# Removing the two zero columns between and behind the token streams: 384 columns instead of 386, and outer convolution taps per stream

## What is computed

```python
def depthwise_conv(x, w, b):                    # x (batch, tokens, channels), zero padding at both ends
    k = w.shape[0]
    left = (k - 1) // 2
    y = lax.conv_general_dilated(x, w[:, None, :], window_strides=(1,),
                                 padding=[(left, k - 1 - left)], feature_group_count=x.shape[-1], ...)
    return y + b

def conv_ffn(h, w_in, dw, dw_b, w_out):         # all four layers, 3 taps, 1024 -> 2 x 2816 -> 1024
    u = depthwise_conv(h @ w_in, dw, dw_b)
    return (jax.nn.silu(u[..., :FFN_DIM]) * u[..., FFN_DIM:]) @ w_out

def ssd_mixer(h, ...):                          # layer 1, 3 taps
    proj = h @ w_in
    xbc = jax.nn.silu(depthwise_conv(proj[..., SSD_D_INNER:SSD_D_INNER + SSD_CONV_DIM], conv_w, conv_b))
    ...
```

## Time and profile before

| | |
|---|---|
| median of 3 runs | 1994.08 us (1992.12 to 1994.34) |
| the profiled execution, its own time | 1993.56 us |
| its span in the trace | 1991.8 us |
| PE busy | 1925.1 us, 97% of the span |
| DVE, ACT, POOL busy | 58%, 47%, 35% |
| mean granted TensorE clock | 0.988 |

### The profile page before, as it was taken

How to read it: one execution, slowest core, us unless ns; L and a number is a source line. 1 busy time by engine, 2 the same in 40 slices (tenths; PEclk the granted TensorE clock), 3 DMA queues, 4 the chain that set the end, 5 groups by cost and what they waited for, 6 DMA issues and landing times.

```text
span 1991.8 us, 30109 instructions
## 1 busy us (share of the span) xinstructions
PE 1925.1 (97%) x11802; PEld 1712.5 (86%) x11802; DVE 1153.4 (58%) x1803; ACT 926.5 (47%) x1575; POOL 697.6 (35%) x507
## 2 busy tenths in 40 slices
PE   5899999999998989999999999999999999999998
PEld 4789998799996767999987967899987977899986
DVE  3657751666626675777714953777723564777722
ACT  3534442544547645544425335544424454544422
POOL 0233334333335553323343741333243521323342
PEclk8999999999999999999999998999999999999999
DMA  9774356543240137634375664634364613443342
GB/s 395 315 271 137 127 183 231 179 119 125 92 135 28 49 138 297 211 119 125 101 259 180 206 184 190 235 125 128 117 219 165 230 39 117 138 123 122 127 127 74
DMA packets 80139, 322.74 MB, mean 162 GB/s; under 512 B 8976, under 2 KB 17664, under 8 KB 66688
## 3 DMA queue, kind: packets, MB, share of 16 engines
q1 hardware_dynamic: 78496, 318.93, 46.7%
q10 hardware_dynamic: 1504, 1.91, 0.3%
HBM read 315.70 MB, written 5.10 MB: 161 GB/s over the span
## 4 chain that ended last, share of the span: by engine, by line
PE 89%; DMA 3%; DVE 3%; issue 2%; ACT 2%; POOL 1%; SPq 0%; DVEq 0%; POOLq 0%; ACTq 0%
PE pair L1968 18%; PE pair L1970 18%; PE pair L1969 18%; PE pair L2001 8%; PE pair L2002 8%; PE pair L2003 8%; DMA mod_base<-in_w_mod 2%; PE pair L2122 2%; PE pair L1935 2%; PE pair L2216 1%; DMA mod_more<-in_w_mod 1%; PE pair L2127 1%; PE pair L1957 1%; PE pair L2136 1%; PE pair L2376 1%
## 5 line engine op out<-in xcount | busy, mean ns | idle before, releaser
L813 POOL TENSOR_TENSOR w_lo<-raw,w_hi 128x512 fp32r<-128x512 f32 (+1 forms) x375 | 588.8, 1572 | 1074.0 <-ACT w_hi L947 1073.9
L1968 PE MATMUL pair<-h_hi,w_hi 128*128 128x386 f32 (+1 forms) x2008 | 688.5, 343 | 3.8 <-DVE h_lo L1467 3.8
L1970 PE MATMUL pair<-h_hi,w_lo 128*128 128x386 f32 (+1 forms) x2008 | 682.9, 340 | 0.0
L1969 PE MATMUL pair<-h_lo,w_hi 128*128 128x386 f32 (+1 forms) x2008 | 682.2, 340 | 0.0
L1361 DVE TENSOR_TENSOR w_lo<-raw,w_hi 128x512 fp32r<-128x512 f32 x339 | 404.3, 1195 | 326.6 <-ACT w_hi L947 326.3
L947 ACT ACTIVATE w_hi<-raw 128x1024 fp32r<-128x1024 f32 x375 | 392.2, 1050 | 281.4 <-PE pair L2003 224.5
L1968 PEld LDWEIGHTS pair<-h_hi,w_hi 128*128 128x128 f32 (+1 forms) x2008 | 380.5, 189 | 12.3 <-issue 11.3
L1969 PEld LDWEIGHTS pair<-h_lo,w_hi 128*128 128x128 f32 (+1 forms) x2008 | 381.0, 190 | 0.5
L1970 PEld LDWEIGHTS pair<-h_hi,w_lo 128*128 128x128 f32 (+1 forms) x2008 | 380.2, 189 | 0.3
L1526 DVE SCALAR_TENSOR_TENSOR acc<-pair,taps,acc 128x385 f32<-128x385 f32 x176 | 108.9, 619 | 202.2 <-ACT acc L1061 202.2
L1061 ACT ACTIVATE acc<-pair,taps 128x386 f32<-128x386 f32 x176 | 117.1, 665 | 217.8 <-PE pair L1970 217.8
(11 more groups left out here) (308 smaller groups left out, 2083.0 us busy)
## 6 DMA issues: line engine op xcount, KB each, us to landing
raw<-in_ffn_in SPq DMA_DIRECT2D x176, 512.0 KB, 3.5
raw<-in_ffn_out SPq DMA_DIRECT2D x88, 512.0 KB, 3.6
mod_raw<-in_w_mod SPq DMA_DIRECT2D x36, 1024.0 KB, 7.1
mod_base<-in_w_mod SPq DMA_DIRECT2D x31, 1024.0 KB, 7.2
mod_more<-in_w_mod SPq DMA_DIRECT2D x18, 1024.0 KB, 21.7
raw<-in_ssd_conv SPq DMA_DIRECT2D x32, 512.0 KB, 3.5
raw<-in_ssd_z SPq DMA_DIRECT2D x16, 512.0 KB, 3.5
raw<-in_ssd_out SPq DMA_DIRECT2D x16, 512.0 KB, 3.5
```

The source lines that it names most:

```text
L813: pool.tensor_tensor(w_lo[:, m % SLOTS, 0:w], raw[:, m % SLOTS, 0:w], w_hi[:, m % SLOTS, 0:w].bitcast(F32), ALU.subtract).then_inc(w_low_p ...
L1968: ten.matmul(to, wh, h_hi[:, k, cols], start=k == 0, stop=False, skip_group_check=True)
L1969: ten.matmul(to, wh, h_lo[:, k, cols], start=False, stop=False, skip_group_check=True)
L1970: ins = ten.matmul(to, wl, h_hi[:, k, cols], start=False, stop=k == KD - 1, skip_group_check=True)
```

## The change

The two zero columns go: `LAT0` is `CTX`, `COLS` is 384, `AT` is 0, 128, 256. Every row of activations, every stream of `tile` and every instruction over a whole row is 384 columns wide; a row of four-byte values is 1536 bytes long, where it was 1544. With no zero between the streams, each outer tap is written for each stream by itself: two instructions over 127 and 255 columns in place of one over 385. The pooling matrices lose the column for the gap, and the four small writes of zeros at the start go.

```diff
-LAT0 = CTX + 1
-COLS = CTX + 1 + LAT + 1
+LAT0 = CTX
+COLS = CTX + LAT
...
             act.wait_ge(cond_loaded, 16)
-            act.wait_ge(vec_init, 2)
+            act.wait_ge(vec_init, 1)
...
                     vec.wait_ge(acc_ready, c + 1)
-                    vec.scalar_tensor_tensor(out=acc[:, j % 4, 1:COLS], in0=b[:, 0:COLS - 1], scalar=taps[:, l, j, 0:1],
-                                             in1=acc[:, j % 4, 1:COLS], op0=ALU.mult, op1=ALU.add).then_inc(tap_first, 1)
+                    for c0, w, _ in STREAMS:
+                        ins = vec.scalar_tensor_tensor(out=acc[:, j % 4, c0 + 1:c0 + w], in0=b[:, c0:c0 + w - 1],
+                                                       scalar=taps[:, l, j, 0:1], in1=acc[:, j % 4, c0 + 1:c0 + w], op0=ALU.mult,
+                                                       op1=ALU.add)
+                    ins.then_inc(tap_first, 1)
...
                     vec.wait_ge(tap_first, c + 1)
-                    vec.scalar_tensor_tensor(out=acc[:, j % 4, 0:COLS - 1], in0=b[:, 1:COLS], scalar=taps[:, l, j, 2:3],
-                                             in1=acc[:, j % 4, 0:COLS - 1], op0=ALU.mult, op1=ALU.add).then_inc(conv_done, 1)
+                    for c0, w, _ in STREAMS:
+                        ins = vec.scalar_tensor_tensor(out=acc[:, j % 4, c0:c0 + w - 1], in0=b[:, c0 + 1:c0 + w],
+                                                       scalar=taps[:, l, j, 2:3], in1=acc[:, j % 4, c0:c0 + w - 1], op0=ALU.mult,
+                                                       op1=ALU.add)
+                    ins.then_inc(conv_done, 1)
...
             vec.memset(cond32[:, :, :], 0.0).then_inc(vec_init, 1)
-            vec.memset(h_hi[:, :, CTX:LAT0].bitcast(F32), 0.0)
-            vec.memset(h_hi[:, :, COLS - 1:COLS].bitcast(F32), 0.0)
-            vec.memset(h_lo[:, :, CTX:LAT0].bitcast(F32), 0.0)
-            vec.memset(h_lo[:, :, COLS - 1:COLS].bitcast(F32), 0.0).then_inc(vec_init, 1)
```

More of the change, by code:

```diff
@@ L1555, in ssd_conv @@
                     vec.wait_ge(acc_ready, c + 1)
-                    vec.scalar_tensor_tensor(out=xbc[:, j, 1:COLS], in0=b[:, 0:COLS - 1], scalar=ssd_taps[:, j, 0:1],
-                                             in1=xbc[:, j, 1:COLS], op0=ALU.mult, op1=ALU.add).then_inc(tap_first, 1)
-                    vec.wait_ge(tap_first, c + 1)
-                    vec.scalar_tensor_tensor(out=xbc[:, j, 0:COLS - 1], in0=b[:, 1:COLS], scalar=ssd_taps[:, j, 2:3],
-                                             in1=xbc[:, j, 0:COLS - 1], op0=ALU.mult, op1=ALU.add).then_inc(conv_done, 1)
+                    for c0, w, _ in STREAMS:
+                        ins = vec.scalar_tensor_tensor(out=xbc[:, j, c0 + 1:c0 + w], in0=b[:, c0:c0 + w - 1],
+                                                       scalar=ssd_taps[:, j, 0:1], in1=xbc[:, j, c0 + 1:c0 + w], op0=ALU.mult,
+                                                       op1=ALU.add)
+                    ins.then_inc(tap_first, 1)
+                    vec.wait_ge(tap_first, c + 1)
+                    for c0, w, _ in STREAMS:
+                        ins = vec.scalar_tensor_tensor(out=xbc[:, j, c0:c0 + w - 1], in0=b[:, c0 + 1:c0 + w],
+                                                       scalar=ssd_taps[:, j, 2:3], in1=xbc[:, j, c0:c0 + w - 1], op0=ALU.mult,
+                                                       op1=ALU.add)
+                    ins.then_inc(conv_done, 1)
                     low_to(s.n0 + j + 5)
@@ L1781, in normed @@
                                                        scalar=attn_tab[:, g:g + 1],
-                                                       in1=bank(6 + i % 2)[:, col - (col > 0):col - (col > 0) + w],
+                                                       in1=bank(6 + i % 2)[:, col:col + w],
                                                        op0=ALU.mult, op1=ALU.mult)
@@ L2511, in pool_matrices @@
         for n in (CTX, LAT):
-            f = np.zeros((n, n + 1), np.float32)
+            f = np.zeros((n, n), np.float32)
             for t in range(n):
```

## The result

The changed kernel takes 1959.32 us (median of 4 runs, 1959.02 to 1961.35), the kernel before beside it 1994.21 us (1992.12 to 1994.51). The ratio is 0.9827, with a 95% interval of 0.9815 to 0.9839: 34.9 us faster. The forecast was 11.3 us, and its range ended at 1979.0. The direction was right, the size a third of what came.

The account below looks back on a forecast made before the run. PE was taken to bound the kernel, more than half through products of `tile`. Narrower products give 11.3 us, split taps on DVE 0, so 1994.08 becomes 1982.8 us; range 1979 to 1993.

Parts of the forecast that it names:

- PE bounds the kernel: Whole kernel: PE busy 97% of the span; 6024 tile products at 177.2 ns from start to start make 54%.
- The stationary pieces of `out_part` start elsewhere in a row: Products of `out_part`: their stationary operands begin at other places, count and width unchanged, claimed worth 0.
- The width term: Products of `tile`: streaming 384 columns instead of 386 saves 1.88 ns each, over 6024 products 11.3 us.
- the step would then be 175.35: Products of `tile`: start-to-start time at 384 columns, claimed to fall from 177.23 to 175.35 ns.
- The line through 256 and 512 columns: PE products: price of 0.4465 ns a column from two full widths; 386 columns measured 1.0 ns above it.
- Pieces of 16 bytes: Streams of `tile`: 386 columns cost as if fetched four columns at a time, the last fetch half empty.
- DVE hidden: Outer taps on DVE: splitting adds 0.12 to 0.20 us a tap, 50 to 83 us, none of it lengthening the kernel.
- The idle time of 1.22 us: DVE's wait before every second tile, claimed to fall from 1.22 to about 0.65 us and not to nothing.
- the margin forecast as 0.19 us or more: End of `ffn_in`: time left between the last tile's second tap and PE needing that bank, from 0.59 us before.
- the case of DVE as the bound: Rival: a tap split costing over 0.28 us makes DVE and ACT slower than PE; 2024 us, chance 0.06.
- only the slope: Rival: in `tile` the 1.0 ns excess stays, two columns save 5.3 us, giving 1988.8 us; chance 0.27.
- the step stays: Rival: 24 loads and their place beside the streams set a tile's pace; 1994 us within a few, chance 0.15.

## Why the prediction was wrong, point by point

**PE bounds the kernel, and the step from start to start is its price**: right. Both terms of the gain, and the loss of nearly every experiment, come out of steps times counts.

**"The stationary pieces of `out_part` start elsewhere in a row, with nothing in their count or width changed: 0"**: wrong, and the larger of the misses, 12.4 us. The count of a kind of product and its width were taken for all that its price can hang on. The earlier trace rows had shown a step of the same width that was 1.1 ns shorter, and I used that only as doubt about the tile; after the change the same half-wide tile takes 173.1 ns, and the difference is 0.2. The run with rows of `g` 385 columns apart shows that the row length alone makes 226.8 or 232.8 ns.

**The width term, 1.88 ns, 11.3 us**: the size came out, 1.95 ns with rows and places of before and 2.2 on average with all alike, but that was in good part luck. It was worked out as the distance to a line that was no floor (next point), from a cost paid in every product; with all alike 386 columns cost 0.1 ns in one tile and 4.3 in the next.

**That the step would then be 175.35**: wrong by 2.0 ns, 12 us. The line through 256 and 512 columns was taken as the floor, but both of its points had been measured in the kernel before, where operands did not lie alike. After the change the 512-wide step is 226.8 and the settled 256-wide one 120.0 (118.2 before), and (226.8 - 120.0) / 256 = 0.417 ns is the cycle of a 2.4 GHz clock. On that line 384 columns are 173.4, what was measured. The 0.4465 ns a column of the prediction held 5.7 ns of misplacement at its upper end, and its lower end was 1.8 ns too fast. I did note that rows of 1544 bytes begin at odd places, but as another name for the same 1.0 ns above the line, not as a cost of its own.

**Pieces of 16 bytes**: not what the place is about. The Trainium skill (SBUF — State Buffer, Specifications (TRN2)) has lines of 16 bytes; rows of 388 columns keep to them in every place and still take 174.7 ns where 173.4 was to be had. For the width, the alternating tiles of 386 columns speak against a half-empty last piece; 384, 256 and 512 are multiples of many things, and 386 is the only other width that ran, so what makes a width good stays open.

**DVE hidden**: right. The timeline of DVE over two tiles of the first `ffn_in`, which answers to the earlier trace rows:

```profile
261.76 0.74 DVE L1527 SCALAR_TENSOR_TENSOR acc<-pair,taps,acc 128x127 f32<-128x127 f32 x2 [1.15 <-ACT acc L1061]
262.41 0.55 DVE L1533 TENSOR_TENSOR g<-gate,g 128x384 fp32r<-128x384 f32 x1
262.88 0.74 DVE L1537 SCALAR_TENSOR_TENSOR acc<-pair,taps,acc 128x127 f32<-128x127 f32 x2
263.53 1.14 DVE L1361 TENSOR_TENSOR w_lo<-raw,w_hi 128x512 fp32r<-128x512 f32 x1
265.62 0.74 DVE L1527 SCALAR_TENSOR_TENSOR acc<-pair,taps,acc 128x127 f32<-128x127 f32 x2 [0.96 <-ACT acc L1061]
```

A split tap takes 0.65 us to the next start, as the pooling pair had said (0.66). The idle time of 1.22 us went to 0.96, not to 0.65: four taps take some 0.48 us and the faster PE 0.19, but `w_lo` gives 0.40 back. It takes 1.40 us in the odd tile of a pair, where it took 1.64, and 1.14 in the even one, where it took 1.30. Over the run `w_lo` on DVE fell from 403.8 to 362.3 us, which is why DVE's busy time rose by 9.7 us and not by the 50 to 83 of the prediction; without it the rise is 51. In the run with unsplit taps it is 404.9 us again, so the gain comes with the split; how was not shown. At the end of `ffn_in` the margin forecast as 0.19 us or more is there, PE first and then DVE:

```profile
273.04 0.39 PE L2009 MATMUL pair<-w_hi,g 128*128 128x512 f32 x1
...
275.80 0.39 PE L2009 MATMUL pair<-w_hi,g 128*128 128x512 f32 x1
```

```profile
274.72 0.74 DVE L1537 SCALAR_TENSOR_TENSOR acc<-pair,taps,acc 128x127 f32<-128x127 f32 x2
```

The last tap ends at 275.46, and c = 0 begins at 275.80, 2.76 us after the first product of `ffn_out` (forecast 2.78). The taps of both streams in one instruction gave the same time, so the case of DVE as the bound is out.

**The rivals and the range**: "only the slope" and "the step stays" both fell, on the other side. What was missing is a rival below the forecast. I had the mechanism in hand: the rival of the unchanged step speaks of 24 loads "and their place beside the streams" and says that such an effect "can go either way". But I gave the side of a larger gain 2 in 100 and priced the effect for tiles alone. The same 1.1 ns of the earlier trace rows over all 8184 products would have put 9 us below the forecast into the range, and the true time still more than 14 us outside it.

## What to carry to other kernels

When a change alters the length of a row or of a buffer, it moves every operand behind it; list where the operands of the costliest products begin, relative to each other modulo 256 bytes, before and after, and count a few ns for each product either way. Where single steps of a product stream scattered in a fixed pattern (177.2, 176.0, 175.6 ns), an even pace of 173.4 was to be had, and a line drawn through scattered steps was no floor; an even pace need not be the floor either (120.0 and 113.3 ns for 256 columns). Rows whose length is a multiple of 256 bytes, with all operand buffers at one offset, were as good as any arrangement tried here for products of 384 and 512 columns and for the whole kernel, and a pad of 64 bytes is a cheap way to find out. Read single steps too and not their mean alone: a mean of 175.6 was 173.5 and 177.6 by turns.

## What the runs showed of the hardware that I had not expected

- Two unused pads of 64 bytes between operand buffers cost 15.6 us of 1959 (0.8%); moving only the weights by 128 bytes cost 28.1 us (1.4%); moving everything by 64 cost nothing.
- With all operands alike, a product took its columns at 2.4 GHz plus 13.3 to 13.4 ns, at 256, 384 and 512 columns; with the weights 192 bytes ahead, one of 256 took 6.7 ns more than its columns. The Trainium skill (TensorE: Matmul & The Clock Gate, Back-to-back issue gap) has 2.5 ns in its formula for the gap, which it gives for a product by itself and not for a stream with loads like this one; no stream of products with weights read here came nearer than the 6.7.
- Out of step, a 512-wide product took 228.9 to 234.3 ns and a 384-wide one up to 176.7, and at one distance (64 bytes) the same product on the same places ran at 173.3 in one stage and 174.7 in another.
- Products of 386 columns, all operands alike, ran at 173.5 ns in one tile and 177.6 in the next, where 384 columns took 173.4 throughout.
